# Reordering VectorE's work ahead of an attention stage, and where three waits for PSUM banks stand

## The reference

```python
h = layer_norm(x, ln_in_g, ln_in_b)
proj = h @ w_in                       # u_pool | u_conv | c_q | c_kv | k_r | gate logits
u_pool, u_conv, c_q, c_kv, k_r, g_logits = split(proj)
y_pool = pool_mixer(u_pool) @ pool_proj   # windowed means of 2, 4, 8, 16 tokens, minus u, 4 groups of 128 channels
y_conv = conv_module(u_conv) @ conv_proj  # a * sigmoid(gate), causal depthwise conv of 31 taps, norm, silu
q = rms_norm(c_q) @ w_uq              # 8 heads of 64 plain + 32 rotary columns
k_nope, v = split(rms_norm(c_kv) @ w_ukv)
q_rope, k_rope = apply_rope(q_rope), apply_rope(k_r)
y_mla = attention([q_nope, q_rope], [k_nope, k_rope], v) @ mla_proj    # 8 heads, chunk-causal mask
merged = g0 * y_pool + g1 * y_conv + g2 * y_mla
```

## Time and profile before

| | |
|---|---|
| median of 3 runs | 2576.95 us (2573.79 to 2578.36) |
| the profiled execution, its own time | 2578.36 us |
| span of its trace, first to last instruction | 2576.5 us |
| PE busy | 2521.8 us (98% of the span) |
| VectorE busy | 1344.4 us (52%) |
| ScalarE busy | 603.5 us (23%) |
| GpSimd busy | 84.7 us (3%) |

### The profile page before, as it was taken

The page is one execution under the profiler, slowest core; times in us unless marked ns, Lnnn a source line. Parts: engine busy times, 40 slices in busy tenths (PEclk is TensorE's granted clock), DMA queues, the critical chain, the costliest instruction groups (busy, mean ns, idle before and its releaser), DMA issues.

```text
span 2576.5 us, 31115 instructions
## 1 busy us (share of the span) xinstructions
PE 2521.8 (98%) x10560; PEld 1876.2 (73%) x10560; DVE 1344.4 (52%) x2465; ACT 603.5 (23%) x1364; POOL 84.7 (3%) x117
## 2 busy tenths in 40 slices
PE   7999999999999999999999999999999999999998
PEld 6856767684444457888746888888885658888886
DVE  6786553341111127647285777753361757777633
ACT  3244112120000003213232322210231623222112
POOL 0010000000000010000030000000000100000000
PEclk9999999999999999999999999999999999999999
DMA  3214222247999952222212222223322012222233
GB/s 141 82 67 179 90 74 82 91 167 285 362 333 335 337 201 69 83 91 82 72 51 91 82 90 86 85 90 131 106 90 75 9 57 98 82 90 90 85 119 122
DMA packets 90382, 319.01 MB, mean 124 GB/s; under 512 B 9584, under 2 KB 13680, under 8 KB 90256
## 3 DMA queue, kind: packets, MB, share of 16 engines
q1 hardware_dynamic: 81408, 284.37, 31.1%
q10 hardware_dynamic: 5152, 19.92, 1.9%
q0 software_dynamic: 3728, 13.44, 1.6%
HBM read 295.61 MB, written 22.02 MB: 123 GB/s over the span
## 4 chain that ended last, share of the span: by engine, by line
PE 93%; DVE 4%; issue 1%; ACT 1%; DMA 0%; ACTq 0%; DVEq 0%
PE bank L871 44%; PE bank L600 13%; PE bank L1064 13%; PE bank L843 4%; PE bank L979 3%; PE bank L723 2%; PE bank L745 2%; PE bank L772 1%; PE bank L1339 1%; PE bank L1327 1%; PE bank L1209 1%; PE bank L755 1%; DVE R L2830 1%; PE bank L634 1%; PE bank L1076 1%
## 5 line engine op out<-in xcount | busy, mean ns | idle before, releaser
L871 PE MATMUL bank<-SQ,arena 128*128 128x256 f32 x2040 | 468.1, 379 | 0.0
L871 PEld LDWEIGHTS bank<-SQ,arena 128*128 128x128 f32 x2040 | 387.5, 190 | 52.8 <-DVE arena L1991 0.2
L1064 PE MATMUL bank<-arena 128*128 128x512 f32 x768 | 336.1, 597 | 3.0 <-ACT arena L1666 1.9
L871 PE MATMUL bank<-X,ring 128*128 128x256 f32 x1360 | 322.5, 379 | 0.0
L600 PE MATMUL bank<-arena,ring 128*128 128x256 f32 (+1 forms) x1280 | 319.7, 411 | 2.6 <-DVEq L2450 1.6
L600 PEld LDWEIGHTS bank<-arena,ring 128*128 128x128 f32 x1280 | 243.0, 190 | 78.2 <-issue 47.5
L871 PEld LDWEIGHTS bank<-X,ring 128*128 128x128 f32 x1360 | 258.2, 190 | 42.6 <-issue 8.4
L1064 PEld LDWEIGHTS bank<-arena 128*128 128x128 f32 x768 | 145.7, 192 | 180.7 <-issue 180.7
L2013 DVE TENSOR_TENSOR bank<-bank,arena 128x256 f32<-128x256 f32 x97 | 41.9, 432 | 242.2 <-ACT bank L1533 241.9
L871 PE MATMUL bank<-SQ,ring 128*128 128x256 f32 x680 | 160.8, 379 | 1.2 <-DVE R L2018 0.9
L871 PE MATMUL bank<-X,arena 128*128 128x256 f32 x680 | 160.7, 379 | 0.0
(11 more groups left out here) (367 smaller groups left out, 2952.1 us busy)
## 6 DMA issues: line engine op xcount, KB each, us to landing
ring<-w_stream SPq DMA_DIRECT2D x338, 512.0 KB, 3.2
arena<-w_stream SPq DMA_DIRECT2D x192, 512.0 KB, 5.6
y_slots<-X ACTq DMA_DIRECT2D x1, 9216.0 KB, 26.1
y_slots<-arena ACTq DMA_DIRECT2D x16, 512.0 KB, 6.8
X<-x_t SPq DMA_DIRECT2D x2, 1024.0 KB, 7.3
x_tok<-arena ACTq DMA_DIRECT2D x1, 2048.0 KB, 6.6
out_t<-X SPq DMA_DIRECT2D x16, 128.0 KB, 2.2
part<-params SPq DMA_DIRECT2D x1, 824.0 KB, 10.4
```

The costliest lines, as they stand in the source:

```text
L871: mm = pe.matmul(out, w(n), v(k), start=start and n == 0, stop=n == len(chunk_pairs(p)) - 1, skip_group_check=not start)
L1064: mm = pe.matmul(bank[t % 4][:, :], w_, ERING[:, at:at + S], start=(k == 0), stop=(k == len(lhs) - 1))
```

## The change

Four edits, of which the second and third go together:

1. `shared_banks` no longer waits for the three other banks; `begin` waits for all four before its first product. This concerns only the first pair of stages "in" and "gates".
2. On DVE, taps 57 to 61 move ahead of `pool_mix(0)`; `pool_mix(2)` and `pool_mix(3)` move ahead of the rotary part of the queries; and taps 62 to 71 (ten, where there were six) stand between the pool mixes and the rotary part.
3. The "gates" stage runs four taps fewer: the groups begin at tap 72 instead of 68, and its seventh pair (p = 6) has one group of four left where it had two.
4. GpSimd, before it copies the queries of heads 0 and 1, waits for the ACT copies of the key tiles uk0 to uk3 instead of those of the query tiles uq0 to uq3.

```diff
--- before.py
+++ after.py
@@ -820,9 +820,6 @@
 
                     if plain:
                         pe.wait_ge(st_out, st_at("out", stage, plain, 0))
-                    else:
-                        for n in range(1, 4):
-                            m_read(pe, T0[AFTER[stage]] + n - 4)
                     for out in (b, c):
                         pe.matmul(out, ident, cstt[:, 0:H], start=True, stop=True)
 
@@ -854,7 +851,8 @@
                     slab = n0 + each * p
                     fresh = first and stage in ("in", "gates")
                     if fresh:
-                        m_read(pe, T0[AFTER[stage]] - 4)
+                        for n in range(4):
+                            m_read(pe, T0[AFTER[stage]] + n - 4)
                     else:
                         pe.wait_ge(st_out, st_at("out", stage, p, -1, i))
                     for n in (slab, slab + 1):
@@ -2331,7 +2329,7 @@
             LAST_QUARTER = (MSG[:, 0, H:S], MSG[:, 1, H:S], CQ[:, 1, H:S], CKV[:, 0, H:S], UP[:, 0, 16 + H:16 + S],
                             KT[:, 1, H:S], UP[:, 2, 16 + H:16 + S])
 
-            TAPS_IN = (10, 9, 8, 8, 9, 9, 4, 0)
+            TAPS_IN = (10, 9, 8, 8, 9, 9, 4, 5)
             conv_taps(0, TAPS_IN[0])
             for p in range(7):
                 if p == 5:
@@ -2359,7 +2357,7 @@
                     dve.tensor_tensor(KR, KT[:, 0], KT[:, 1], ALU.add).then_inc(k_rope_in, 1)
                 conv_taps(sum(TAPS_IN[:p + 1]), sum(TAPS_IN[:p + 2]))
 
-            def pool_mix(g):
+            for g in range(4):
                 if g == 3:
                     m_read(dve, T0["in"] + 4)
                 else:
@@ -2385,10 +2383,7 @@
                     .then_inc(pool_mixed, 1)
                 dve.wait_ge(pool_mixed, g + 1)
 
-            pool_mix(0)
-            pool_mix(1)
-            conv_taps(57, 62)
-            conv_taps(62, 68)
+            conv_taps(62, 72)
             QH = ATT["att"]["QH"]
             for r in range(2):
                 t = T0["uq"] + 4 + 2 * r
@@ -2404,8 +2399,6 @@
                     q = slice(32 * j, 32 * j + 32)
                     dve.tensor_tensor(QH[64:96, 4 * r + j], RT[q, 0], RT[q, 1], ALU.add).then_inc(rope_q, 1)
                 dve.wait_ge(rope_q, 4 * r + 5)
-            pool_mix(2)
-            pool_mix(3)
             attention("att")
 
             def merge(n):
@@ -2432,11 +2425,11 @@
                     merge(2 * p - 2)
                     merge(2 * p - 1)
                 if p < 7:
-                    conv_taps(68 + 8 * p, 72 + 8 * p)
+                    conv_taps(72 + 8 * p, min(76 + 8 * p, 4 * TAPS))
                 third_sum("gates", p)
                 fourth_output("gates", p, GS[:, 2 * (p % 2) + 1, H:S])
                 if p < 7:
-                    conv_taps(72 + 8 * p, 76 + 8 * p)
+                    conv_taps(min(76 + 8 * p, 4 * TAPS), min(80 + 8 * p, 4 * TAPS))
                 if p == 6:
                     sync()
                     dve.engine_nop().then_inc(merged, 1)
@@ -3021,7 +3014,7 @@
 
             pool.wait_ge(rope_q, 9)
             for j in range(4):
-                m_read(pool, T0["uq"] + j)
+                m_read(pool, T0["uk"] + j)
 
             def latent_values():
                 for j in range(4):
```

## The result

The changed kernel is slower: median 2592.31 us of five executions (2585.79 to 2592.67) against 2576.98 us, ratio 1.0051, 95% interval 1.0035 to 1.0067. In a second measurement it had a median of 2588.63 us (2584.48 to 2592.52, six executions), ratio 1.0044, interval 1.0032 to 1.0056. Together the eleven have the median 2589.34. Its profiled execution took 2588.62 us, 10.26 more than that of before; the forecast for this comparison was 10.7. Its times lie at separate levels, 2584 to 2586, 2588 to 2589 and above 2592. The levels go with the clock: the mean granted clock of an execution is 0.996 or 0.997 at the lowest level, 0.994 or 0.995 at the middle one and 0.993 in the four executions above 2592.

A forecast was written before the change was run, and what follows sets the result against it. PE was taken as the bound, busy 2521.8 of 2576.5 us. 7.8 us (edits 2 to 4), 0.8 (clock) and 2.1 (edit 1) sum to 10.7 over the 2576.95 median: 2587.7 us, range 2583.5 to 2592.5.

The forecast's parts named there:

- Edits 2 and 3: VectorE order before the query rotary part: two mixes and four taps more delay the uq4 read 11.2 us, the stage 5.7.
- The stop of PE: On PE between uq7 and uk0: idle from 170.4 to 175.1 us, 4.7 us, until VectorE has read uq4.
- cover of 6.6 us: At uq4's bank, which PE takes again at 170.4: VectorE's read could be 6.6 us late before PE stops.
- The freed maxima: Head 0 maxima on VectorE, no longer behind the moved mixes: nothing gained, as PE has values matmuls until 186.2 us.
- Edit 4: GpSimd query copy waiting for the key copies, ahead of `scores(0)`: 2.1 us of the 7.8; 1.2 alone behind the new order.
- Edit 1: First products of "in" and "gates" waiting for all four banks: 1.0 and 1.1 us later, 2.1 us in all.
- The clock: PE clock falls once at uk0 behind the long stop, costing 1.7 us, of which 0.8 remain; bounds 0 and 2.5.
- The sum: Whole kernel: 7.8 + 0.8 + 2.1 = 10.7 us, giving 2587.7 us against the median; chance 0.74.
- (b): Rival at the first products of "in" and "gates": waits cost nothing and no clock fall; 7.8 us, 2584.8; chance 0.07.
- (c): Rival on VectorE before the uq4 read: the stretch is shorter in its new place; 2582 us; chance 0.05.
- (d): Rival at the head 0 maxima: the mixes ahead of them hold the attention; 4.6 us gained, 2572.3; chance 0.02.
- rival (a): Clock falls more than once, behind `scores(0)` and in the attention, up to 1.7 us each; 2591.1 us; chance 0.12.

## Why the prediction was right

- **PE is the bound, and lateness on it goes through.** Right: 10.30 us of useless PE work moved the median by 10.1 us.
- **Edits 2 and 3.** The stretch of VectorE from the key rotation to the read of uq4 was to be about 25.5 us and is 25.10 (151.01 to 176.11). The read was to move by 11.2 us; measured against uq0 it moved from 13.41 to 24.20, 10.8. The stop of PE was to be 4.7 us and was 4.17. uq6 was to be waited for, and is where the clock stays up. That four taps and two mixes must be taken together, behind a cover of 6.6 us, is shown by the two parts: 0.0 us and 3.2 us alone, 6.15 together, the fall included. The freed maxima and the taps of "gates" gained nothing, as said; over 200 us of "gates" (241 to 441) PE is busy for 199.73.
- **Edit 4.** Forecast 2.1 of the 7.8 us as the distance from uk3 to the scores; it is 2.11 us of idle. That VectorE would be idle, and the copy short, held: 1.27 us for two. The 1.2 us that the prediction gave as the worth of this edit behind the new order are too few: it is 2.3 (35.88 less 33.61), since the fall at uk0 hides the copy under the old wait.
- **Edit 1.** 1.0 and 1.1 us forecast, 1.2 and 1.25 measured. The mis-sized term is the signal from ACT to PE: 0.1 us forecast, 0.31 measured at both places. (The idle in the brackets, 1.01 and 1.10, is less than the lateness because two matmuls in a row overlap in the profile by some 0.15 us.)
- **The clock.** One fall at uk0, of which 0.8 us would remain: it came, in both traces of the changed kernel, and filling the stop won 0.9. The second fall around `scores(0)`, the upper end of this term, was not in either trace, but edit 4 alone shows two falls behind such a stop in one of its traces.
- **The sum.** 10.7 us against 10.9 by the landmarks: 8.6 against 8.42 from uq0 to `scores(0)`, and 2.1 against 2.4 for edit 1, so two small misses cancel. That the two profiled executions lie 10.26 us apart is partly luck, since the falls elsewhere can differ by more than that agreement is close.
- **The rivals.** (b), (c) and (d) are refuted. (The 2582 of (c) is 5 us above before; 5 us off the forecast would be 2582.7.) The first median, 2592.31, is that of rival (a) rather than of the forecast, and only 0.2 us inside the upper end of the range, which was luck; the second, 2588.63, is the forecast's. The falls that (a) named, one behind `scores(0)` and one in the attention that follows, are in neither trace. What the forecast lacked is that the number of falls in the rest of the kernel varies: the times of the changed kernel lie 8.2 us apart, which is some five falls of 1.7 us (an estimate), so that a median of five can stand on one level or the other. I had taken 1.5 us for the runs' own scatter.
- **Still open.** What decides in one execution how many falls come, and whether the changed kernel's times near 2592 are due to the stop ahead of `scores(0)`. Filling both stops removed them from five executions, no more.

## What to carry to other kernels

In a kernel whose main engine has no gap, ask of every reordering on a helper engine how long the cover is behind the first result that is awaited from it: here 6.6 us, under which work is free. Above it the work counts at least in full: 1.3 us over the cover cost 3.2, and 4.2 over it cost 6.15. Moving work ahead of what PE waits for, to free a place where it waits for nothing, gains nothing at best. A few microseconds between medians should be checked against the granted clock of the traces: subtract the loss first, then compare landmarks.

## What the runs showed that was not expected

- The same kernel lost 3.4 us to the clock in one execution and 8.5 in another; over all traces it was 1.8 to 10.3 us, mostly in steps of 1.7. Most falls lie not behind the stops of 2 us and more, but around the router's 16-column matmuls (near 530 to 570 us), in the experts and in the last attention.
- Taps beside POOL's key copies take 4.80 us for five, 0.96 each, and 0.67 without (5.38 for eight). The eight POOL copies take 8.12 us, 1.02 each, so it goes about one tap a copy. Three pool additions take 2.18 us now and took 2.76 beside POOL's query copies. The Trainium skill (SBUF — State Buffer, "Who interferes with whom") states that a VectorE instruction with two SBUF inputs contends with a GpSimd instruction that reads SBUF, and calls the contention for their shared ports an exclusive lock. The trace agrees by this pace; nothing here tells such a lock from a shared rate.
